# Moving the matmul operands by multiples of 64 bytes within SBUF, with the weights left in place

## What is computed

```
for layer in (0, 1):                      # first block
    mod = split(silu(c) @ ada_w[layer] + ada_b[layer], 6)
    h = rms(x) * (1 + mod[1]) + mod[0]    # also of the context
    y = h @ w_in ... mixer ... @ w_out    # layer 0: convolution + mLSTM, layer 1: latent attention
    x = x + mod[2] * y
    x = x + mod[5] * conv_ffn(rms(x) * (1 + mod[4]) + mod[3])
for l in (0, 1):                          # second block
    h = rms_norm(x, norm_mix_pre[l])
    m = hybrid_mixer(h @ w_in_2[l])       # differential + dilated attention, gated, @ w_out_2[l]
    x = x + rms_norm(m, norm_mix_post[l])
    x = x + rms_norm(swiglu(rms_norm(x, norm_ffn_pre[l])), norm_ffn_post[l])
```

## Time and profile before

| | |
|---|---|
| median of 2 runs | 3673.74 us (3673.59 to 3673.9) |
| the profiled execution | 3674.51 us |
| its span, first to last instruction | 3672.7 us |
| TensorE busy | 3572.8 us (97%), mean granted clock 0.995 |
| VectorE, ScalarE, GpSimd busy | 1983.1, 1620.1, 1325.2 us |
| mean DMA rate | 91 GB/s |

### The profile page before, as it was taken

How to read it: one execution, slowest core, us unless ns; L and a number is a source line. 1 busy time by engine, 2 the same in 40 slices (tenths; PEclk the granted TensorE clock), 3 DMA queues, 4 the chain that set the end, 5 groups by cost and what they waited for, 6 DMA issues and landing times.

```text
span 3672.7 us, 56483 instructions
## 1 busy us (share of the span) xinstructions
PE 3572.8 (97%) x21302; PEld 2938.1 (80%) x21302; DVE 1983.1 (54%) x3008; ACT 1620.1 (44%) x2819; POOL 1325.2 (36%) x614
## 2 busy tenths in 40 slices
PE   7999999999999999999999999999999999999998
PEld 5875788888877777888777778789977777878997
DVE  4857553333357775343555653557555665356555
ACT  4344432221266663332655552445455555335444
POOL 2530333232331113444422334355543233344555
PEclk9999999999999999999999999999999999999999
DMA  5368221111220002322312222232322222222332
GB/s 211 115 230 309 92 75 63 63 63 63 69 81 24 24 24 91 99 97 92 102 59 70 70 70 94 77 105 87 115 87 69 70 70 70 86 93 75 110 104 92
DMA packets 85382, 335.84 MB, mean 91 GB/s; under 512 B 9648, under 2 KB 9776, under 8 KB 78640
## 3 DMA queue, kind: packets, MB, share of 16 engines
q1 hardware_dynamic: 84448, 330.79, 26.7%
q10 hardware_dynamic: 720, 2.10, 0.2%
HBM read 329.18 MB, written 2.10 MB: 90 GB/s over the span
## 4 chain that ended last, share of the span: by engine, by line
issue 44%; PE 36%; POOL 14%; DVE 3%; ACT 1%; POOLq 0%; DMA 0%; ACTq 0%; DVEq 0%; SPq 0%
POOL w_lo L3550 14%; PE pB L287 7%; PE pB L288 7%; PE pB L289 6%; PE pT L1095 2%; PE pT L1096 1%; PE pT L1097 1%; PE pT L289 1%; PE pT L288 1%; PE pT L287 1%; PE pO L287 1%; PE pO L289 1%; PE pO L288 1%; PE pO L1097 1%; PE pO L1095 1%
## 5 line engine op out<-in xcount | busy, mean ns | idle before, releaser
L3550 POOL TENSOR_TENSOR w_lo<-w_raw,w_hi 128x1024 fp32r<-128x1024 f32 x452 | 1106.9, 2452 | 2071.2 <-ACT w_hi L333 2070.1
L333 ACT ACTIVATE w_hi<-w_raw 128x1024 fp32r<-128x1024 f32 x452 | 476.5, 1055 | 561.0 <-PE pB L289 365.0
L287 PE MATMUL pB<-h_hi,w_hi 128*128 128x512 f32 x1540 | 607.7, 395 | 18.7 <-DVE h_lo L477 6.0
L288 PE MATMUL pB<-h_lo,w_hi 128*128 128x512 f32 x1540 | 600.3, 390 | 0.0
L289 PE MATMUL pB<-h_hi,w_lo 128*128 128x512 f32 x1540 | 599.5, 389 | 0.0
L287 PE MATMUL pB<-b_hi,w_hi 128*128 128x512 f32 (+1 forms) x1084 | 399.2, 368 | 3.6 <-DVE b_lo L1307 1.6
L288 PE MATMUL pB<-b_lo,w_hi 128*128 128x512 f32 (+1 forms) x1084 | 394.9, 364 | 0.0
L289 PE MATMUL pB<-b_hi,w_lo 128*128 128x512 f32 (+1 forms) x1084 | 394.6, 364 | 0.0
L287 PEld LDWEIGHTS pB<-h_hi,w_hi 128*128 128x128 f32 x1540 | 290.0, 188 | 94.4 <-issue 15.5
L289 PEld LDWEIGHTS pB<-h_hi,w_lo 128*128 128x128 f32 x1540 | 289.8, 188 | 61.0
L288 PEld LDWEIGHTS pB<-h_lo,w_hi 128*128 128x128 f32 x1540 | 290.1, 188 | 58.0 <-issue 1.2
(11 more groups left out here) (673 smaller groups left out, 7085.1 us busy)
## 6 DMA issues: line engine op xcount, KB each, us to landing
w_raw<-stream SPq DMA_DIRECT2D x520, 512.0 KB, 3.3
under<-ada SPq DMA_DIRECT2D x42, 1024.0 KB, 5.6
arena<-ada SPq DMA_DIRECT2D x6, 1024.0 KB, 17.4
x<-xT SPq DMA_DIRECT2D x1, 2048.0 KB, 9.2
out<-x SPq DMA_DIRECT2D x8, 256.0 KB, 2.1
xc<-cT SPq DMA_DIRECT2D x1, 1024.0 KB, 26.5
arena<-bmask ACTq DMA_DIRECT2D x1, 1024.0 KB, 4.9
w_hi<-arena SPq DMA_DIRECT2D x4, 192.0 KB, 8.4
```

The source lines that it names most:

```text
L287: pe.matmul(dst, lh, rh, start=(begin and k == 0), stop=False)
L288: pe.matmul(dst, lh, rl, start=False, stop=False)
L333: act.activation(w_hi[:, s, :], w_raw[:, s, :], ACT.Copy).then_inc(hi_ready, 1)
L3550: pool.tensor_tensor(w_lo[:, s, :], w_raw[:, s, :], w_hi[:, s, :].bitcast(F32), ALU.subtract).then_inc(lo_ready, 1)
```

## The change

Each of the four operand tensors gets an unused 64 bytes in front of it; 768 unused bytes follow b_lo, so that the weights and all after them lie 1024 bytes further on. Another 320 unused bytes stand in front of the arena, and 64 bytes each in front of xh_lo, xb_hi and xb_lo. The overlay under grows with the pads, and two slices of it are cut to their old length. No instruction is added, removed or moved to another engine.

```diff
--- before.py
+++ after.py
@@ -149,10 +149,13 @@
             pass
         xc = sb("xc", [P, KD, C])
 
-        with nc.sbuf_tensor("under", [P, 4, KD * T], F32) as under:
+        sb("place_h", [P, 16])
+        with nc.sbuf_tensor("under", [P, 4, KD * T + 16], F32) as under:
             pass
-        h_hi, h_lo = sb("h_hi", [P, KD * T], F32R), sb("h_lo", [P, KD * T], F32R)
-        b_hi, b_lo = sb("b_hi", [P, KD * T], F32R), sb("b_lo", [P, KD * T], F32R)
+        h_hi, _ = sb("h_hi", [P, KD * T], F32R), sb("place_h_lo", [P, 16])
+        h_lo, _ = sb("h_lo", [P, KD * T], F32R), sb("place_b_hi", [P, 16])
+        b_hi, _ = sb("b_hi", [P, KD * T], F32R), sb("place_b_lo", [P, 16])
+        b_lo, _ = sb("b_lo", [P, KD * T], F32R), sb("place_w", [P, 192])
         w_raw = sb("w_raw", [P, SLOTS + 1, KD * P])
         w_hi, w_lo = sb("w_hi", [P, SLOTS, KD * P], F32R), sb("w_lo", [P, SLOTS, KD * P], F32R)
         w_hi6, w_lo6 = sb("w_hi6", [P, HALF_K], F32R), sb("w_lo6", [P, HALF_K], F32R)
@@ -170,6 +173,7 @@
         cond_sb = sb("cond_sb", [P, 2 * KD])
         cond_pad = sb("cond_pad", [P, KD, 32])
         lam_junk = sb("lam_junk", [P, 64])
+        sb("place_arena", [P, 80])
         with nc.sbuf_tensor("arena", [P, ARENA], F32) as arena:
             pass
         with nc.sbuf_tensor("mla_under", [P, 5376], F32), nc.sbuf_tensor("mla_q", [P, 4, T], F32R) as mla_q, nc.sbuf_tensor("mla_k", [P, 4, TC], F32R) as mla_k:
@@ -177,9 +181,11 @@
         with (nc.sbuf_tensor("below_t", [P, 3072], F32), nc.sbuf_tensor("arena_t", [P, 1024], F32R) as arena_t,
               nc.sbuf_tensor("between_t", [P, 9216 - 4096], F32), nc.sbuf_tensor("arena_u", [P, 512], F32R) as arena_u):
             pass
-        xh_hi, xh_lo = sb("xh_hi", [P, KD * C], F32R), sb("xh_lo", [P, KD * C], F32R)
-        xb_hi, xb_lo = sb("xb_hi", [P, KD * C], F32R), sb("xb_lo", [P, KD * C], F32R)
-        sb("arena_rest", [P, ARENA - 4 * KD * C])
+        xh_hi, _ = sb("xh_hi", [P, KD * C], F32R), sb("place_xh_lo", [P, 16])
+        xh_lo, _ = sb("xh_lo", [P, KD * C], F32R), sb("place_xb_hi", [P, 16])
+        xb_hi, _ = sb("xb_hi", [P, KD * C], F32R), sb("place_xb_lo", [P, 16])
+        xb_lo = sb("xb_lo", [P, KD * C], F32R)
+        sb("arena_rest", [P, ARENA - 4 * KD * C - 48])
         pB = ctx.enter_context(nc.psum_tensor("pB", [P, 1024], F32))
         pB2 = ctx.enter_context(nc.psum_tensor("pB2", [P, 512], F32))
         bank = [pB[:, 0:512], pB[:, 512:1024], pB2[:, :]]
@@ -528,7 +534,7 @@
 
         n_ada = LAYERS * ADA_M // ADA_G * KD
         half = KD * T // 2
-        spare = [under[:, 1, 0:half], under[:, 2, half:], under[:, 3, half:]]
+        spare = [under[:, 1, 0:half], under[:, 2, half:KD * T], under[:, 3, half:KD * T]]
         turned = under[:, 0, 0:512]
         ada_bank = [bank[0]] + [bank[2]] * 5
         ADA_BANK_FREE = (0, 0, 2, 3, 4, 5)
```

## The result

| | before | after |
|---|---|---|
| median of the runs | 3673.74 us | 3711.52 us (3710.44 to 3712.6, 2 runs) |
| ratio | 1 | 1.0103, 95% interval 1.0074 to 1.0133 |
| span of the profiled execution | 3672.7 us | 3708.6 us |
| mean granted clock | 0.995 | 0.996 |

The kernel became 1% slower, within the 2% that count as no change; the likeliest case of the prediction was 2.4% faster. The time is that of rival C. One of the ten executions of a later kernel (the context's half alone) ran at a mean granted clock of 0.653 and took 5055 us; it is left out of that kernel's median.

The account below looks back on a forecast made before the run. TensorE's matmul spacing was taken to bound the kernel; 65.4 us from 512 columns and 24.0 us from 256, sum 89.4 us, took 3674.5 to 3585.1, against the median 3584 us; range 3518 to 3715.

Parts of the forecast that it names:

- rival C: Wide matmuls of h and b: distances changing at each matmul never settle, spacing stays 231 ns; 3710 us, chance 0.17.
- the likeliest case of the prediction: Rival A, all moved matmuls: every distance other than 0 is worth about 6.7 ns; 3584 us, chance 0.37.
- What bounds the kernel: Whole kernel: TensorE busy 97% of the span; time is matmuls times the distance between starts, plus untouched stages.
- Addresses matter: Seven-product stage, 256 columns: spacing depends on distance from the weights, 120 ns at 0 against 113 at 192.
- Rival D: Moved tensors: 64 to 256 bytes act like 0, only 192 or its tensors are cheap; 3674 us, chance 0.12.
- the price of a wide matmul: 512-column matmuls at a new distance: 6.7 ns gain each, taken from 256-column rows; bounds 13.3 ns gain or loss.
- The term of -65 us: 512-column matmuls with a new distance: 9756 x 6.7 ns = 65.4 us gained.
- The 256-column term: 256-column matmuls with a new distance: 3576 x 6.7 ns = 24.0 us gained.
- Counting modulo 512: All operands: distance from the weights counted modulo 512 bytes, as one weight block of 128 columns is 512 bytes long.
- Rival B: Moved matmuls: partial gain, collision returning at 128 or 256 or mixed distances settling between; 3606 to 3660 us, chance 0.27.
- Unchanged tensors: attP_t and xc_t keep their distances, so durations stay at 277 and 283 ns; if they move, counting by distance is wrong.
- Plain f32, pads, DMAs, other engines: Attention and transposes, allocations, weight loads, ScalarE, VectorE and GpSimd: costed at nothing; plain f32 at most 2 us.

Follow-up runs that it names:

- the context's half alone: Only the change's pads in front of and inside the arena, against the kernel before; h, b and weights as before: 3669.83 us, ratio 0.9988.
- the pair of pads of 64 and 256 bytes: Against the kernel before, four pads ahead of h_hi, h_lo, b_hi and b_lo, arena distances kept: 64 bytes each 1.0104, 256 bytes each 3673.14 us, 0.9995.
- the 64-byte grid: Small kernels without the model, TensorE alone, triples for each pair of hi and lo distances: 226.7 ns at 0 with 0 for 512 columns, 120.0 for 256.
- the two halves of the change: Against the kernel before, only the pads of the four wide parts (3713.54 us, 1.0104), then only those of the arena (3669.83 us, 0.9988).
- the context at 192 bytes: Against the kernel before, the arena with the context's four parts 192 bytes on; h, b and weights as before: 3667.20 us, ratio 0.9979.

## Why the prediction was wrong, point by point

- **What bounds the kernel: right.** TensorE's spacing sets the time. All of the change is in it, no wait was added, and no other engine moved.
- **Addresses matter: right. Nothing else in the change did anything.** Rival D, no effect at all, fell by the pair of pads of 64 and 256 bytes.
- **The step that failed: the price of a wide matmul.** "I take for both lengths the 6.7 ns between the xc_t and the attP_t rows, as the excess at distance 0 is the same 13.3 ns for both lengths." An equal excess at distance 0 said nothing of the other distances. For 256 columns 0 is the dearest of the 64-byte grid (120.0 ns, 192 alike being 113.3 or 117.8), for 512 it is the cheapest (226.7, 192 alike being 233.3): the sign turns with the length. The term of -65 us came out as +45 (26.8 + 18.7): 110 of the 127 us between 3584 and 3711.5.
- **The 256-column term: right sign, too large.** -24.0 us was predicted; the four rows of 256 columns of h, b, xh and xb above give -4.8 (-6.1 without the long distances of b). The step of one pair of distances (0 to 192) was applied to all; most distances give 117.8, and 113.3 came only where hi and lo stand alike, and there not every time.
- **Counting modulo 512: wrong.** The period is 256 bytes. That the block of weights is 512 bytes long was a guess at the cause. b_lo was rightly at 0, but xh at (320, 384) was (64, 128) and not far places of their own.
- **Rival C: the time right (3710 against 3711.5), the reason wrong.** It blamed distances that alternate and a sequence that never settles. One pair at 192 without any alternation costs 233.3 ns, and the dear spacings are lasting patterns, not a failure to settle. That unlike distances add something of their own is true of 192 with 0 (234.5). The 231 ns of the earlier trace rows, from which C was priced, happened to be near what h's layout costs. Its -7 us for the narrow matmuls was near the -4.8.
- **Rival B and the mixture of the earlier trace rows:** 118 ns for a mixture was taken as "mixing loses most of the gain". In the grid 117.8 is what most layouts at 256 columns cost, mixed or alike.
- **Unchanged tensors: wrong in one.** "attP_t and xc_t must stay at 277 and 283." attP_t did; xc_t went to 281, though its distance is as it was. It has an h product for a neighbour, and h had moved. From start to start it went from 120.0 to 118.4 ns in the change, to 118.4 with the pads of h and b alone, and stayed at 120.0 with the context's alone. By the prediction's own sign this makes its count by distance wrong; the distance counts, but it is not all: what ran before counts too.
- **Plain f32, pads, DMAs, other engines: nothing, as said.**

Left open: the mechanism below the patterns. In the small kernels the steps repeat after 3, 6, 9 or more matmuls, and where I could make out the repeat at distances in multiples of 16 bytes it took, with one exception, a multiple of 6.667 ns, which is 16 cycles of 2.4 GHz: three matmuls 680.0 ns at a mean of 226.67, 686.7 at 228.89, 693.3 at 231.11, and six 1400 at 233.33. Which fetch waits for which, and why 256 bytes, no run shows.

## What to carry to other kernels

Take a price only from a row with the same shape: here the same move of 192 bytes gained 6.7 ns at 256 columns and lost 6.7 ns at 512. Before a layout is changed for TensorE's sake, measure triples at the distances in question in a kernel that does nothing else, each from the predecessor it will really have; it took some 22 us a case, and its prices foretold the two halves of the change and the pads of 256 bytes to 0.1%. They missed the context at 192 bytes by 6 us (3661 expected, 3667.20 measured), where the real kernel fell into the dearer of two patterns. And try the distance that should do nothing (256 bytes here) beside the one that should do something.

## What the hardware showed that I had not expected

- Float32r matmuls with a weight load for each have lasting spacings from 226.7 to 240.0 ns at 512 columns and 113.3 to 123.3 at 256, at a granted clock of 1.00 and with all other engines idle. In steps of 64 bytes they go by the distance between weights and moving columns, with a period of 256 bytes (within 0.1 ns at 512 columns).
- Some layouts have more than one such pattern (113.3 and 117.8; 228.9 and 233.3; 233.3 and 236.7), and the matmuls before decide which, down to the pattern that they themselves were in.
- Shorter weights shift the pattern and do not simply help: at 512 moving columns and distance 0, 32 columns of weights took 231.7 ns and 128 took 226.7; at 192, 96 took 228.3 and 128 took 233.3.
- Off multiples of 64 bytes the address counts by itself: with all operands moved on by 16 bytes the spacing went from 226.7 to 233.3 ns, by 240 bytes to 231.1.
